# A state space layer computed over blocks of four tokens

## The reference

```python
u = h @ w_in_c                                   # (T, 1024) = 64 groups of 16 channels
ar, ai = mag * cos(li * dt), mag * sin(li * dt)  # pole of each of 64 groups x 64 states
bb = z * B                                       # complex, z from the pole
x = einsum('btgc,gpc->btgp', u, bb)              # complex input; x[0] += a * s0
s[t] = a * s[t-1] + x[t]                         # complex scan over the tokens
y = einsum('btgp,gcp->btgc', s, C).real + d_skip * u
mix = (gelu(y) @ w_glu_v) * sigmoid(gelu(y) @ w_glu_g)
```

## Time and profile before

| | us |
|---|---|
| Three runs | 2927.67, 2928.01, 2933.19 (median 2928.01) |
| The profiled execution | 2928.22 |
| Its span, first to last instruction | 2926.5 |
| PE busy (matmuls) | 2744.6 (94%) |
| DVE busy | 1681.6 (57%) |
| ACT busy | 1116.7 (38%) |
| POOL busy | 370.9 (13%) |

### The profile page before, as it was taken

The page is one execution under the profiler, slowest core; times in us unless marked ns, Lnnn a source line. Parts: engine busy times, 40 slices in busy tenths (PEclk is TensorE's granted clock), DMA queues, the critical chain, the costliest instruction groups (busy, mean ns, idle before and its releaser), DMA issues.

```text
span 2926.5 us, 50984 instructions
## 1 busy us (share of the span) xinstructions
PE 2744.6 (94%) x18105; PEld 2684.2 (92%) x18105; DVE 1681.6 (57%) x2781; ACT 1116.7 (38%) x1438; POOL 370.9 (13%) x545
## 2 busy tenths in 40 slices
PE   7999999999999999999999813999999999999997
PEld 7999998999999999999999701799999999999997
DVE  7656665555554555455555687665554555455554
ACT  5544454333333333333333210444443343334432
POOL 1323332210000000000013271220000000000011
PEclk9999999999999999999999956999999999999999
DMA  6444444445545554455445400254555555455543
GB/s 175 127 117 126 138 124 118 138 135 145 143 138 143 145 142 137 144 149 143 141 133 147 106 0 1 81 144 139 148 146 145 154 144 147 144 153 147 147 140 96
DMA packets 739192, 382.64 MB, mean 131 GB/s; under 512 B 13560, under 2 KB 734756, under 8 KB 739140
## 3 DMA queue, kind: packets, MB, share of 16 engines
q1 hardware_dynamic: 722352, 365.34, 44.0%
q0 software_dynamic: 2560, 7.29, 1.1%
q10 hardware_dynamic: 14228, 9.31, 1.1%
HBM read 373.31 MB, written 8.57 MB: 130 GB/s over the span
## 4 chain that ended last, share of the span: by engine, by line
PE 85%; DVE 7%; issue 3%; ACT 2%; ACTq 1%; DVEq 1%; POOL 0%; DMA 0%; SPq 0%; POOLq 0%
PE banks L1410 27%; PE banks L1411 26%; PE banks L1412 26%; ACT wh L477 1%; DVE wl L900 1%; PE banks L1717 1%; DVE banks L389 1%; DVE xs L390 1%; DVE m1v L388 1%; DVE SB L1119 1%; PE bank L1549 1%; PE bank L1557 1%; PE bank L1717 0%; PE bank L1475 0%; POOL ZP L407 0%
## 5 line engine op out<-in xcount | busy, mean ns | idle before, releaser
L900 DVE TENSOR_TENSOR wl<-raw,wh 128x1024 fp32r<-128x1024 f32 x708 | 888.1, 1255 | 916.9 <-ACT wh L477 916.2
L1410 PE MATMUL banks<-h,wh 128*128 128x336 f32 (+1 forms) x3648 | 1161.7, 318 | 13.4 <-DVE U L1291 4.1
L1411 PE MATMUL banks<-h,wh 128*128 128x336 f32 (+1 forms) x3648 | 1151.6, 316 | 0.0
L1412 PE MATMUL banks<-h,wl 128*128 128x336 f32 (+1 forms) x3648 | 1149.3, 315 | 0.0
L477 ACT ACTIVATE wh<-raw 128x1024 fp32r<-128x1024 f32 x708 | 748.6, 1058 | 965.2 <-PE banks L1412 950.7
L1410 PEld LDWEIGHTS banks<-h,wh 128*128 128x128 f32 x3648 | 689.3, 189 | 18.3 <-DVE wl L900 4.4
L1411 PEld LDWEIGHTS banks<-h,wh 128*128 128x128 f32 x3648 | 688.7, 189 | 3.3 <-issue 1.7
L1412 PEld LDWEIGHTS banks<-h,wl 128*128 128x128 f32 x3648 | 688.8, 189 | 0.0
L1410 PE MATMUL banks<-act,wh 128*128 128x322 f32 (+1 forms) x1872 | 592.0, 316 | 9.3 <-DVE GA L1000 3.2
L1411 PE MATMUL banks<-act,wh 128*128 128x322 f32 (+1 forms) x1872 | 589.1, 315 | 0.0
L1412 PE MATMUL banks<-act,wl 128*128 128x322 f32 (+1 forms) x1872 | 587.3, 314 | 0.0
(11 more groups left out here) (362 smaller groups left out, 1807.1 us busy)
## 6 DMA issues: line engine op xcount, KB each, us to landing
raw<-in_w_up SPq DMA_DIRECT2D x172, 512.0 KB, 3.9
raw<-in_w_gate SPq DMA_DIRECT2D x172, 512.0 KB, 3.9
raw<-in_w_down SPq DMA_DIRECT2D x160, 448.0 KB, 3.6
raw<-in_w_in_e SPq DMA_DIRECT2D x96, 512.0 KB, 3.8
raw<-in_w_out_e SPq DMA_DIRECT2D x32, 512.0 KB, 3.8
raw<-in_w_down SPq DMA_DIRECT2D x32, 512.0 KB, 3.9
raw<-in_w_in_c SPq DMA_DIRECT2D x16, 512.0 KB, 4.0
raw<-in_w_glu_v SPq DMA_DIRECT2D x16, 512.0 KB, 3.9
```

The lines of the kernel that those rows point to most:

```text
L900: v.tensor_tensor(wl[:, j % RING, :], raw[:, j % RING, :], wh[:, j % RING, :].bitcast(F32), ALU.subtract) \
L1410: pe.matmul(out, whi, hi, start=first and k == 0, stop=False)
L1411: pe.matmul(out, whi, lo, start=False, stop=False)
L1412: ins = pe.matmul(out, wlo, hi, start=False, stop=last and k == kn - 1)
```

## The change

Tokens are taken in blocks of four (`STEP`). For each block the input matmuls make no longer every token's input but what the block adds to the state at its end: four accumulated matmuls, with B, AB, A^2B and A^3B against the four tokens. Each of the four positions of a block has `BLK` = 26 columns (17 chunks, 8 samples and one more) in three or four blocks, `XW` = 104 columns. The scan then has three steps inside a chunk, and the carry loop is kept with A^16. The output of position t of a block is C A^(t+1) against the state before the block (tables CT1 to CT4), plus kernels C A^j B against the block's own tokens (table K5, with d_skip on its diagonal). `spread` adds the carried state at three of the four block ends of a chunk, so no products go to PE for all 16 positions. POOL scans nothing. ACT writes the gelu straight out of PSUM.

The tables: the parameters' loads on POOL start when the first feed-forward starts, and the pole arithmetic, the transposes of poles, C and states, B2 and C's first tables are made under `down` of its part 1, whose first five bodies are unrolled for it (`poles`). U5 is cleared by POOL when `win` starts (`u5_zero`), and POOL makes the powers of B during `win`; PE turns them and multiplies them with C (`tables`) behind four of the sixteen tiles.

```diff
-POOL_PAIRS = 8
-DVE_PAIRS = PAIRS - POOL_PAIRS
+STEP = 4
+BLK = 2 + CH + NS
+XW = STEP * BLK
+QUARTER = PAIRS // 4
 DEAD = META - 2
...
+        def times_power(eng, st, src, k, r, first, second, out):
+            other = 2 * r if out is BX else 2 - 2 * r
+            eng.tensor_tensor(first, src[:, r], power(k, 1), ALU.mult)
+            st.then(eng.tensor_tensor(second, src[:, 1 - r], power(k, other), ALU.mult))
+        def into_blocks(eng, r, first, second, out):
+            for g in range(2):
+                rowsl = slice(g * P5, (g + 1) * P5)
+                plane = out[:, r] if out is BX else out[:, :, r, :]
+                to = plane.rearrange("p j (q g c) -> p j q g c", q=4, g=2)[rowsl, :, :, g, :]
+                view = lambda t: t[rowsl].rearrange("p (j q) c -> p j q c", q=4)
+                ins = eng.tensor_tensor(to, view(first), view(second), ALU.add)
             return ins
...
+        def take_x(copy, j):
+            src = wide[j % 2]
+            dst = xs[:, :, 4 * j:4 * j + 4, :].rearrange("p r q x -> p q r x")
+            x = src[:, :, 0:2 * XW].rearrange("p q (r x) -> p q r x", r=2)
+            copy(dst[:, :, :, BLK:BLK + 1 + PCH], x[:, :, :, 0:1 + PCH])
+            copy(dst[:, :, :, 2 * BLK:XW], x[:, :, :, BLK:3 * BLK])
+            return copy(dst[:, :, :, 0:BLK], x[:, :, :, 3 * BLK - 1:XW - 1])
...
+            for j in (0, 2, 4, 5, 6, 7):
+                e.wait_ge(x5, j + 1)
+                take_x(lambda to, x: sc.activation(to, x, ACT.Copy), j).then_inc(x5a, 1)
+            e.wait_ge(scan5, 2)
...
+            e.wait_ge(c0_made, 1)
+            for n, to in ((1, CT1), (2, CT2)):
+                st.then(gp.memset(to[:], 0.0))
+                for r in range(2):
+                    times_power(gp, st, C0, n - 1, r, cp[:], cq[:], to)
+                    st.then(into_blocks(gp, r, cp, cq, to))
+            squares(PH["down02"], (0, 1), 2)
...
+            for k in range(1, STEP):
+                times_power(gp, st, B2, k - 1, 0, bp[:], bq[:], BX)
+                gp.tensor_tensor(ip, B2[:, 1].rearrange("p (j q) c -> p j q c", q=4), power(k - 1, 1).rearrange("p (j q) c -> p j q c", q=4), ALU.mult)
+                st.then(gp.tensor_tensor(iq, B2[:, 0].rearrange("p (j q) c -> p j q c", q=4),
+                                         power(k - 1, 2).rearrange("p (j q) c -> p j q c", q=4), ALU.mult))
+                e.wait_ge(bx_used, k)
+                into_blocks(gp, 0, bp, bq, BX)
+                for g in range(2):
+                    rowsl = slice(g * P5, (g + 1) * P5)
+                    to = BX[:, 1].rearrange("p j (q g c) -> p j q g c", q=4, g=2)[rowsl, :, :, g, :]
+                    ins = gp.tensor_tensor(to, ip[rowsl], iq[rowsl], ALU.add)
+                ins.then_inc(bx_made, 1)
+                e.wait_ge(bx_made, k + 1)
+            e.wait_ge(evac, PH["glu"].group(0, 0) + BANK_CREDIT)
...
+                if (b, j) == (2, 3):
+                    e.wait_ge(t5, 1)
+                    az = bank[2][:, 0:4 * PAIRS].rearrange("p (k n) -> p k n", k=4)
+                    v.tensor_copy(AP5[:, 1, 0, :], az[:, 0, :])
+                    v.tensor_copy(AP5[:, 2, 0, :], az[:, 1, :]).then_inc(a_made, 1)
+                    zb = lambda k: az[:, 2 + k, :].unsqueeze(2).to_broadcast([P, PAIRS, C5])
+                    v.tensor_tensor(B2[:, 0], Bn[:, 0], zb(0), ALU.mult)
+                    st.then(v.tensor_tensor(B2[:, 1], Bn[:, 1], zb(1), ALU.mult))
+                    st.then(v.tensor_tensor(B2[:, 0], B2[:, 0], B2[:, 1], ALU.subtract))
+                    v.tensor_tensor(B2[:, 1], Bn[:, 1], zb(0), ALU.mult)
+                    st.then(v.tensor_tensor(Bn[:, 0], Bn[:, 0], zb(1), ALU.mult))
+                    v.tensor_tensor(B2[:, 1], B2[:, 1], Bn[:, 0], ALU.add).then_inc(b2_made, 1)
...
+            def scan_half(half):
+                q = slice(16 * half, 16 * half + 16)
+                for i in range(1, 4):
+                    n = PCH if i == 1 else PCH + NS
+                    prev, cur = (xs[:, :, q, BLK * k + 1:BLK * k + 1 + n] for k in (i - 1, i))
+                    A0 = AP5[:, 1:2, 3, q].unsqueeze(3).to_broadcast([P, 2, 16, n])
+                    A1 = AP5[:, 0::2, 3, q].unsqueeze(3).to_broadcast([P, 2, 16, n])
+                    m = lambda t: t[:, :, 0:16 * n].rearrange("p r (q c) -> p r q c", c=n)
+                    v.tensor_tensor(m(m0), A0, prev, ALU.mult)
+                    st.then(v.tensor_tensor(m(m1)[:, ::-1], A1[:, ::-1], prev, ALU.mult))
+                    st.then(v.tensor_tensor(m(m0), m(m0), m(m1), ALU.add))
+                    if i < 3:
+                        st.then(v.tensor_tensor(cur, cur, m(m0), ALU.add))
+                    else:
+                        e.wait_ge(x5, 8)
+                        v.tensor_tensor(SC[:, :, :, q].rearrange("p c r q -> p r q c"), cur[:, :, :, 0:PCH], m(m0)[:, :, :, 0:PCH], ALU.add)
+                        v.tensor_tensor(cur[:, :, :, PCH:n], cur[:, :, :, PCH:n], m(m0)[:, :, :, PCH:n], ALU.add).then_inc(scan5, 1)
+                        e.wait_ge(scan5, half + 1)
...
+            def spread(u):
+                q = slice(u * QUARTER, (u + 1) * QUARTER)
+                full = [P, 3, CH, QUARTER]
+                for r in range(2):
+                    S = lambda k: SC[:, 0:CH, k, q].unsqueeze(1).to_broadcast(full)
+                    A = lambda plane: AP5[:, plane, 3:6, q].unsqueeze(2).to_broadcast(full)
+                    v.tensor_tensor(sp5[:, r, 0], A(1), S(r), ALU.mult)
+                    ins = v.tensor_tensor(sp5[:, r, 1], A(2 * r), S(1 - r), ALU.mult)
+                st.then(ins)
+                for r in range(2):
+                    ins = v.tensor_tensor(sp5[:, r, 0], sp5[:, r, 0], sp5[:, r, 1], ALU.add)
+                st.then(ins)
+                for r in range(2):
+                    to = xs[:, r, q, 0:3 * BLK].rearrange("p q (i x) -> p i x q", x=BLK)[:, :, 2:2 + CH, :]
+                    ins = v.tensor_tensor(to, to, sp5[:, r, 0], ALU.add)
+                ins.then_inc(spread5, 1)
...
+            def tables(k):
+                e.wait_ge(bx_made, k + 1)
+                if k:
+                    e.wait_ge(bt_c, 4 * k)
+                for b in range(4):
+                    for m in range(4):
+                        ins = pe.transpose(bank[2 + b][:, m * P:(m + 1) * P], BX[:, b // 2, 4 * (b % 2) + m, :], ident[:])
+                    ins.then_inc(bt_t, 1)
+                for j in range(8):
+                    for r in range(2):
+                        for q in range(4):
+                            ins = pe.matmul(bank[6][32 * q:32 * q + 32, (8 * k + j) * C5:(8 * k + j + 1) * C5],
+                                            BX[:, r, j, 32 * q:32 * q + 32], C0[:, r, 4 * j + q, :], start=r == 0, stop=r == 1)
+                ins.then_inc(bx_used, 1)
...
             for j in range(8):
+                if j == 2 or j in (4, 5, 6, 7):
+                    e.wait_ge(x5a, {2: 1, 4: 2, 5: 2, 6: 3, 7: 4}[j])
+                if j in (3, 5):
+                    e.wait_ge(x5v, j // 2)
                 for r in range(2):
+                    for t in range(STEP):
+                        for q in range(4):
+                            ins = pe.matmul(wide[j % 2][:, q, r * XW:(r + 1) * XW], BT[32 * q:32 * q + 32, j, STEP - 1 - t, r, :],
+                                            U5[32 * q:32 * q + 32, j, t * XW:(t + 1) * XW], start=t == 0, stop=t == STEP - 1)
+                ins.then_inc(x5, 1)
+            e.wait_ge(k_made, 1)
+            e.wait_ge(x5a, 6)
+            for j in range(8):
+                for t in range(STEP):
                     for q in range(4):
+                        pe.matmul(bank[(4 + j) % 8][32 * q:32 * q + 32, t * XW:STEP * XW], K5[32 * q:32 * q + 32, t, j, :],
+                                  U5[32 * q:32 * q + 32, j, 0:(STEP - t) * XW], start=t == 0, stop=False)
+            e.wait_ge(ct_made, 2)
+            for k in range(8):
+                if k % 2 == 0:
+                    e.wait_ge(spread5, k // 2 + 1)
+                    e.wait_ge(ends5, k // 2 + 1)
+                for t in range(STEP):
                     for r in range(2):
+                        for q in range(4):
+                            ins = pe.matmul(bank[(4 + k) % 8][32 * q:32 * q + 32, t * XW:(t + 1) * XW],
+                                            CTs5[t][:, k, r, 32 * q:32 * q + 32], xs[:, r, 4 * k + q, 0:XW], start=False,
+                                            stop=t == STEP - 1 and r == 1)
+                ins.then_inc(y_made, 1)
```

More of the change, by code:

```diff
@@ L249, in build @@
-        bank += [ctx.enter_context(nc.psum_tensor(f"bank{i}", [P, 512], F32)) for i in range(4, 8)]
+        wide = [ctx.enter_context(nc.psum_tensor(f"banks{4 * i}", [P, 4, 512], F32)) for i in range(2)]
+        bank = [wide[i // 4][:, i % 4, :] for i in range(8)]
         BA = (bank[3], bank[4])
@@ L679, in down @@
                                 hi_of_x(ph, i, j - 2, gnext, i * 2 + j - 2)
```

(35 more changed lines are left out.)

515 lines of the change are left out of this document (225 added, 290 removed).

## The result

The changed kernel takes 2840.7 us (median of 4 runs, 2834.98 to 2842.8) against 2930.07 beside it: ratio 0.9691, 95% interval 0.9673 to 0.971. The forecast was 2851. One execution of a later run (7144.56 us, with TensorE's instructions about twice as long throughout) was a disturbed one and is left out of every comparison.

A forecast was written before the change was run, and what follows sets the result against it. PE bounds the kernel except in a 199.5 us island without weight tiles, where DVE rules. From 2928.22 us, +6 + 21.8 - 105.1 = -77.3 gives 2851 us; own range 2835 to 2866, 8 times in 10 2833 to 2892.

The forecast's parts named there:

- Step 1: Pole tables made under part 1's down projection: +6 us (2.7 if all is covered, +15 if exposed whole).
- The block of (2,3): DVE's pole work behind that tile's split in part 1's down projection: a later add to X about 0.9 us late.
- Step 2: Input projection `win`: 5.6 us removed, four tables of transposes and small matmuls added, +21.8 us (14.1 to 37.5).
- p: Time from one small PE instruction with its weight load to the next: taken as 0.04 us, between 0.022 and 0.07.
- the lower bound: Smallest price of a small PE instruction: 0.022 us for 104 columns streamed, 0.028 where 128 columns of weights are loaded.
- rival A: Small matmuls are issued no faster than 0.062 us, whatever their columns: 2880 us; chance 0.27.
- Step 3: The island from the last `win` matmul to the first of `glu`: 94.4 us against 199.5, -105.1 us.
- C's powers 3 and 4 on POOL ready before 61.8: In the island, POOL's 26 us of work on these is ready before the carry loop's end at 61.8 us.
- own range: The forecast's total for the whole kernel from low ends to high: 2835 to 2866 us.
- C (2956): Every small instruction costs 0.111 us, as weight loads don't go abreast in different groups: +27.6, 2956 us; chance 0.05.
- B (2866): The feeders are late: PE waits for POOL's last BX powers and pole blocks are exposed whole: +15, 2866 us; chance 0.17.

The follow-up runs named there:

- experiment 1: Changed kernel with GpSimd leaving the third and fourth C tables at zero (serves only to time the scan): 2831.93 us, ratio 0.9663.
- experiment 3: Changed kernel with the carry's sixteen steps on VectorE written out in place of a loop: 2829.07 us, ratio 0.9651.
- experiment 4: Changed kernel with table and readout matmuls issued one column group after the other, not in turn: 2868.6 us; run again for a profile, 2866.06 us.
- experiment 5: Changed kernel with the 128 table matmuls behind each of four input projection tiles issued twice, back to back: 2858.21 us, ratio 0.9752.
- experiment 6: Changed kernel with the 128 table matmuls of each of four tables issued a second time, one projection tile later: 2842.47 us, ratio 0.9704.
- experiment 2: Changed kernel with GpSimd making the third and fourth C tables after the scan's second half, beside the carry loop: 2842.97 us, ratio 0.9696.
- experiment 7: Changed kernel with GpSimd's third C table products earlier, VectorE clearing both tables, carry written out, VectorE's pole block moved: 2826.28 us, ratio 0.9642.

## Why the prediction was right, by its steps

The total was right with some luck: 2840.7 for 2851, 10 us low, because one term was much too high and the largest was exact only by errors that cancelled.

**Step 1, +6: measured +6.8** in the profiled execution, and 963.2 to 963.6 us in place of 966.3 in those of experiments 1, 3, 4, 5 and 6 with the same code (966.3 again in experiment 2), so +3.7 to +6.8. The 3 us between the two lie where nothing was changed: in 180 us from 1299 on PE began 1160 matmuls, and 1176 in the same stretch of experiment 3, both at full clock. 28 transposes cost what was said (16 in 1.91 us); the block of (1,1) cost 1.0 to 1.2 us through the late addition to X that the earlier trace rows gave the margin for, as experiment 7 shows, where it is gone. The block of (2,3), for which 0.9 us was counted, cost nothing to be seen.

**Step 2, +21.8: measured +6.7.** This is the term that was mis-sized, by 15.1 us: p was taken as 40 ns and is 10. The form was right: 4 x (1.84 + 1.27) - 5.6 = 6.8. The fault was the lower bound. It was worked out from streams of 104 and loads of 128 columns, and was then used for instructions that stream 16 and load 32; scaled from the same row, 16 columns x 2 passes / 2.4 GHz / 4 groups would have given 3 ns, and the bound for the tables should have been there, apart from the readout's. The rows near 60 ns, on which rival A stood, were streams, as the prediction said; experiment 4 shows 31 ns for one group alone. The measured 10 ns lie between those 3 and the 31, and no run shows what sets them.
The Trainium skill's two figures ("TensorEngine Tiling (Array Packing)", Instruction Overhead: about 60 cycles; "TensorE: Matmul & The Clock Gate", section "Wait — 56ns, not 53.3ns?": starts about 25 ns apart at the closest) don't hold for instructions in four column groups here: 1.27 us for 128. For one group alone, 31 ns, they are near.

**Step 3, -105.1: measured -105.1**, but by terms that cancelled. Against the forecast: scan starts 0.9 us earlier (13.8); first half scan +7.9 (20.0 for 12.1); second half -0.8; carry -0.1; four spreads -3.4 (19.7 for 23.1, their two wide additions take 1.7 us as taken, the rest less); last pair of readout -2.1 (3.0 for 5.1, p again: the 104-column instructions started 22 ns apart at full clock, which was the prediction's own lower bound for them, and 43 at the 1.2 GHz level, its figure for that); tail -0.7. The prediction had "C's powers 3 and 4 on POOL ready before 61.8": they were, and the step that failed is that it looked at when POOL ends and not at what it does to DVE meanwhile. Rows of before don't show that meeting: there each of DVE's scan instructions read one operand from PSUM and the products had 1016 ns for 816 columns in a stretch where POOL was busy for half the time. The half scan's price was taken from those rows and used for instructions that read both operands from SBUF. Two small slips in the sum changed nothing: at p = 0.07 `win` is +37.2 and not 37.5, and 2866 as the upper end of the own range is not what its high ends add up to (with +15 for step 1 they give 2903).

**Rivals.** A (2880) and C (2956) are out by the changed kernel's own rows, 10 ns where they say 62 and 111; even in one group (experiment 4) it is 31. B (2866) had one true part, PE's wait at 1200.76; POOL never kept PE waiting in `win`. By stages the profiled executions differ by 10.7 us from the forecast difference: -15.1 (step 2), +0.8 (step 1), +3.5 (before the change), 0.1.

## What to carry to other kernels

Small matmuls in the four column groups are cheap only if the groups take turns in the innermost loop, and only in short runs between longer work: 128 behind a tile ran through, 256 in a row did not. When work is moved to an idle GpSimd, ask which VectorE instructions it will run beside. Its tensor_tensor work on SBUF cost VectorE about half its own length beside large instructions (8.8 us for 16.5) and two thirds beside small ones (12.4 for 18.4), where VectorE's instructions read both operands from SBUF; where they read one from PSUM, as before the change, it cost nothing. A loop of four tiny dependent instructions on VectorE is worth writing out: here it gave 7.9 us, nearly as much as the contention cost. And before two lengths of the same TensorE work are compared, look at the granted clock of both.

## What the runs showed of the hardware that was not expected

- VectorE and GpSimd on SBUF: 800 columns 0.99 us alone, 1.73 to 2.05 beside GpSimd's tensor_tensor; 64 columns 0.23 alone, up to 1.30. GpSimd's memset (64 columns still 0.22 beside it in experiment 2), VectorE's copies out of PSUM (0.31, 0.58 and 0.36 us with and without GpSimd's work) and the scan of before with one operand in PSUM (1.00 us for 816 columns either way) were not touched.
- TensorE ran 237 fp32 matmuls of 16 columns at 9.2 ns apiece and then stood 2.24 us. All six such pauses end 1.2 to 1.6 us after a 16 KB packet of instructions has landed.
- Other differences in the length of the same TensorE work are the clock's. The 512 input matmuls took 14.55 us in experiment 2 (granted clock 1.00 throughout), 16.18 in the changed kernel (3.4 us of it at 0.50) and 17.43 in experiment 3 (6.1 us at 0.50); 64 of them take 1.79 us at 1.00 in all three. The 128 of the readout take 3.06 us at 1.00 and 4.72 where 3.4 us are at 0.50. Before the input matmuls TensorE had waited the same 3.2 us in all of these; why the clock was low after it in some executions and not in experiment 2, and why it fell in the last readout pair of some, stays open.
